# Long convolution by cosine and sine transforms: the transforms folded by parity of time, on one core

## What is computed

```python
h = (sin(...) @ w3 + b3).reshape(L, HY_ORDER, 2, HY_WIDTH) * window   # filters, forward and backward
f = concatenate([fwd, zeros, bwd[1:][::-1]]); f = f / (sum(abs(f)) + EPS)
spec = jnp.fft.rfft(f, axis=0)                                        # length 2 L
y = jnp.fft.irfft(jnp.fft.rfft(u, n=2 * L) * spec, n=2 * L)[:, :L]    # long_conv(u, spec, skip)
return y + u * skip
v, x1, x2 = split(short_conv(u, conv_w), 3)                           # hyena_mixer
z = x1 * long_conv(v, spec[:, 0], skip[0]);  return x2 * long_conv(z, spec[:, 1], skip[1])
```

## Time and profile before

| | us |
|---|---|
| median of three runs | 3444.6 |
| lowest, highest | 3440.48, 3444.97 |
| profiled execution | 3438.63 |
| its span | 3436.7 |
| TensorE busy | 3308.8 (96%) |
| VectorE busy | 2126.0 (62%) |
| ScalarE busy | 1777.6 (52%) |
| GpSimd busy | 636.9 (19%) |
| mean granted TensorE clock | 0.983 |

### The profile page before, as it was taken

The page is one execution under the profiler, slowest core; times in us unless marked ns, Lnnn a source line. Parts: engine busy times, 40 slices in busy tenths (PEclk is TensorE's granted clock), DMA queues, the critical chain, the costliest instruction groups (busy, mean ns, idle before and its releaser), DMA issues.

```text
span 3436.7 us, 55376 instructions
## 1 busy us (share of the span) xinstructions
PE 3308.8 (96%) x22902; PEld 3047.7 (89%) x22902; DVE 2126.0 (62%) x3208; ACT 1777.6 (52%) x2712; POOL 636.9 (19%) x260
## 2 busy tenths in 40 slices
PE   6889999999999889999999999999999999999999
PEld 6879999998888779999998887888999979899998
DVE  7754956657777556946655555575655456755544
ACT  4434556664444545556654554455455445555562
POOL 0000886660000003976640000000000000000000
PEclk8979999999999999999999999999999999999999
DMA  7343554448887333554456655332534634244355
GB/s 254 129 141 117 160 181 143 139 148 274 278 276 261 129 125 127 180 166 140 142 178 194 197 191 184 129 127 97 186 136 158 186 107 143 86 172 168 120 178 135
DMA packets 263693, 565.53 MB, mean 165 GB/s; under 512 B 15438, under 2 KB 93714, under 8 KB 262674
## 3 DMA queue, kind: packets, MB, share of 16 engines
q1 hardware_dynamic: 263444, 561.99, 50.0%
HBM read 560.89 MB, written 1.05 MB: 164 GB/s over the span
## 4 chain that ended last, share of the span: by engine, by line
PE 84%; DVE 7%; ACT 3%; DMA 3%; POOL 2%; issue 1%; SPq 0%; DVEq 0%; ACTq 0%
PE ps L372 8%; PE ps L1888 8%; PE ps L374 7%; PE ps L1889 7%; PE ps L373 7%; PE ps L1890 7%; PE ps L1970 6%; PE ps L1972 6%; PE ps L1971 6%; PE ps L1936 3%; PE ps L402 3%; POOL uvr_split L2288 2%; PE ps L404 2%; DVE ring_split L471 1%; PE ps L528 1%
## 5 line engine op out<-in xcount | busy, mean ns | idle before, releaser
L2288 POOL TENSOR_TENSOR uvr_split<-uvr,high_split 128x1024 fp32r<-128x1024 f32 x172 | 432.4, 2517 | 1057.8 <-ACT high_split L2017 1057.8
L1890 PE MATMUL ps<-consts_sb_split,uvr_split 128*128 128x256 f32 x2048 | 579.1, 283 | 0.0
L2017 ACT ACTIVATE high_split<-uvr 128x1024 fp32r<-128x1024 f32 x342 | 360.8, 1056 | 235.8 <-PE ps L1972 182.0
L374 PE MATMUL ps<-uvr_split,ring_split 128*128 128x256 f32 x1680 | 476.9, 284 | 0.0
L1889 PE MATMUL ps<-ht_split,high_split 128*128 128x256 f32 x1488 | 423.8, 285 | 0.0
L1888 PE MATMUL ps<-consts_sb_split,high_split 128*128 128x256 f32 x1392 | 403.4, 290 | 6.7 <-DVE ht_split L603 3.8
L471 DVE TENSOR_TENSOR ring_split<-big,high_split 128x2048 fp32r<-128x2048 f32 x111 | 251.8, 2268 | 250.2 <-ACT high_split L463 249.5
L471 DVE TENSOR_TENSOR ring_split<-big,hot_split 128x2048 fp32r<-128x2048 f32 (+2 forms) x111 | 248.6, 2240 | 253.0 <-ACT hot_split L463 252.3
L1971 PE MATMUL ps<-uvr_split,hot_split 128*128 128x512 f32 x1024 | 398.5, 389 | 0.0
L1890 PEld LDWEIGHTS ps<-consts_sb_split,uvr_split 128*128 128x128 f32 x2048 | 392.0, 191 | 0.0
L374 PEld LDWEIGHTS ps<-uvr_split,ring_split 128*128 128x128 f32 x1680 | 323.1, 192 | 0.0
(11 more groups left out here) (462 smaller groups left out, 8433.6 us busy)
## 6 DMA issues: line engine op xcount, KB each, us to landing
uvr<-peer_uv SPq DMA_DIRECT2D x512, 512.0 KB, 4.2
big<-mlp_w SPq DMA_DIRECT2D x32, 2048.0 KB
big<-w_in SPq DMA_DIRECT2D x26, 2048.0 KB
uvr<-mod_w SPq DMA_DIRECT2D x56, 512.0 KB, 6.6
big<-peer_w_q SPq DMA_DIRECT2D x8, 2048.0 KB
big<-hy_w_in SPq DMA_DIRECT2D x6, 2048.0 KB
big<-mod_w SPq DMA_DIRECT2D x24, 512.0 KB, 4.1
big<-mod_w SPq DMA_DIRECT2D x8, 1024.0 KB
```

The source lines that it names most:

```text
L374: m = mm(out, wl, x_high[:, k, :], start=False, stop=en)
L1890: return mm(out, w_low, x_high, start=False, stop=stop, **kw)
L2288: GE.tensor_tensor(expert_low(j), expert(j), expert_high(j).bitcast(F32), ALU.subtract)\
```

## The change

Time steps are taken by parity: "half" `t` of a tile no longer means steps 128 t to 128 t + 127, but even (0) or odd (1) steps. For frequency k and its mirror 255 - k, the sum over even steps is equal and the sum over odd steps changes its sign (cosine; for the sine the even sum changes its sign, and the inverse undoes it). So one product with half of the table is made for each parity, and the sum and the difference of the two results give both halves of the frequencies. The inverse makes sums and differences first, and then one product for each parity of time. Tables shrink to half and are padded to the same size; nothing in the DMA list changes.

What it adds and removes: L2509 and L2684 go from two accumulated products for each (part, k) to one for each (part, parity); the odd one goes to a bank of the pool "act", which ScalarE empties, the even one to a bank of the pool "dve", which VectorE reads directly. L2695 keeps its number of products, each of 128 columns instead of 256. ScalarE empties two banks where it emptied four. VectorE gets `folded_dve` (two instructions on 128x512) for each part, and `sums_by_parity` (two more) for each part of a convolution. The filter functions, transposes and last additions read or write `h2` and `u0` with a step of two elements.

```diff
+        def by_parity_pe(part, src, name):
+            for t, pool in ((1, "act"), (0, "dve")):
+                b = acquire(pool)
+                mm(ps[:, b, :], h_fwd[:, t, part, :], src[t], start=True, stop=True).then_inc(S[filled[pool]], 1)
+                frees(b, "odd_times" if t else name)
+
+        def folded_dve(out, name):
+            even, odd = take("dve"), out[:, 1, :]
+            VE.wait_ge(S["odd_times"], S.nth(VE, "odd_times"))
+            VE.tensor_tensor(out[:, 0, :], even, odd, ALU.add).then_inc(S["dve_step"], 1)
+            VE.tensor_tensor(odd, even, odd, ALU.subtract).then_inc(S[name], 1)
+            VE.wait_ge(S["dve_step"], S.nth(VE, "dve_step"))
+            VE.wait_ge(S[name], S.nth(VE, name))
...
 def filter_pe:
-                    mm(ps[:, b, :], z.h2[0:65, t * P:(t + 1) * P], w[0:65, n * 512:(n + 1) * 512], start=True,
+                    mm(ps[:, b, :], by_parity(z.h2[0:65, :])[:, t, :], w[0:65, n * 512:(n + 1) * 512], start=True,
...
-                    for k in range(2):
-                        b = acquire("act")
-                        for t in range(TM):
-                            m = mm(ps[:, b, :], h_fwd[:, t, part * T + k * P:part * T + (k + 1) * P], src[:, t, o, :],
...
+                    by_parity_pe(part, [src[:, t, o, :] for t in range(TM)], "spectra")
...
 def filter_act:
             magnitudes(2)
-            evict_act(spectra[:2], frees="spectra", n=2)
+            evict_act([z.F[:, 0, w, 1, :] for w in range(2)], frees="odd_times", n=2)
             magnitudes(3)
-            evict_act(spectra[2:4], frees="spectra", n=2)
             split_x_act(h, z.h_high, "h_part")
-            evict_act(spectra[4:], frees="spectra", n=4)
+            evict_act([z.F[:, 1, w, 1, :] for w in range(2)], frees="odd_times", n=2)
...
 def filter_dve:
             block_norm_dve(z.rs, V["ln_mix"][:, 8 * L:8 * L + 8], name="h_part")
+            for w in range(2):
+                folded_dve(z.F[:, 0, w], "spectra")
             magnitudes(2)
             magnitudes(3)
+            folded_dve(z.F[:, 1, 0], "spectra")
             split_x_dve(h, h_low, z.h_high)
+            folded_dve(z.F[:, 1, 1], "spectra")
             split_low()
...
-            VE.wait_ge(S["spectra"], S.nth(VE, "spectra", 8))
...
 def mixers_pe:
-                            for k in range(2):
-                                m = mm(ps[:, b, (c - c0) * T:(c - c0 + 1) * T], z.Y[:, part, k, c * P:(c + 1) * P],
-                                       h_inv[:, 2 * part + k, :], start=(part == 0 and c == c0 and k == 0),
...
+                            for t in range(TM):
+                                at_ = (c - c0) * T + t * P
+                                m = mm(ps[:, b, at_:at_ + P], z.U[:, part, t, c * P:(c + 1) * P],
+                                       h_inv[:, part, t, :], start=(part == 0 and c == c0 and t == 0),
...
 def mixers_act:
-                evict_act([z.U[:, w, k, :] for w in range(2) for k in range(2)], frees="u_spectrum", n=4)
+                evict_act([z.U[:, w, 1, :] for w in range(2)], frees="odd_times", n=2)
...
 def mixers_dve:
-                VE.wait_ge(S["u_spectrum"], S.nth(VE, "u_spectrum", 2))
+                folded_dve(Ur, "u_spectrum")
                 VE.tensor_tensor(z.Y[:, 0], Ur, Fr, ALU.mult).then_inc(S["dve_step"], 1)
                 VE.tensor_tensor(z.Y[:, 1], Ur, Fi, ALU.mult).then_inc(S["dve_step"], 1)
-                VE.wait_ge(S["u_spectrum"], S.nth(VE, "u_spectrum", 2))
+                folded_dve(Us, "u_spectrum")
                 VE.tensor_tensor(z.t1, Us, Fi, ALU.mult).then_inc(S["dve_step"], 1)
                 VE.wait_ge(S["dve_step"], S.nth(VE, "dve_step", 3))
-                VE.tensor_tensor(z.Y[:, 0], z.Y[:, 0], z.t1, ALU.add).then_inc(S["y_spectrum"], 1)
...
+                VE.tensor_tensor(z.Y[:, 0], z.Y[:, 0], z.t1, ALU.add).then_inc(S["dve_step"], 1)
...
+                def sums_by_parity(part):
+                    VE.tensor_tensor(z.U[:, part, 0], z.Y[:, part, 0], z.Y[:, part, 1],
+                        ALU.add).then_inc(S["dve_step"], 1)
+                    VE.tensor_tensor(z.U[:, part, 1], z.Y[:, part, 0], z.Y[:, part, 1],
+                        ALU.subtract).then_inc(S["y_spectrum"], 1)
...
+                sums_by_parity(0)
                 VE.tensor_tensor(z.t1, Us, Fr, ALU.mult).then_inc(S["dve_step"], 1)
                 VE.wait_ge(S["dve_step"], S.nth(VE, "dve_step"))
-                VE.tensor_tensor(z.Y[:, 1], z.t1, z.Y[:, 1], ALU.subtract).then_inc(S["y_spectrum"], 1)
...
+                VE.tensor_tensor(z.Y[:, 1], z.t1, z.Y[:, 1], ALU.subtract).then_inc(S["dve_step"], 1)
...
+                sums_by_parity(1)
```

More of the change, by code:

```diff
@@ L89, in constant_tables @@
     th = 2 * np.pi * (np.arange(T)[None, :] + 0.5) * np.arange(T)[:, None] / (2 * T)
-    fwd = np.concatenate([np.cos(th), np.sin(th)], 1).reshape(TM, P, 2 * T)
-    inv_ = (np.concatenate([np.cos(th), np.sin(th)], 1).T / T).reshape(4, P, T)
+    waves = np.stack([np.cos(th), np.sin(th)], 0)[:, :, 0:P].reshape(2, P, TM, P)
+    fwd = waves.transpose(1, 2, 0, 3)
+    inv_ = waves.transpose(3, 0, 2, 1) / T
+    pad = np.zeros((P, 512))
     tn = np.arange(T, dtype=np.float32) / (T - 1)
@@ L97, in constant_tables @@
     winb[0] = 0.0
[L98 to L100 removed]
+    hy = [fwd.reshape(P, -1), pad, inv_.reshape(P, -1), pad, win.reshape(P, -1), winb.reshape(P, -1)]
     w = (2.0 * math.pi * np.arange(T, dtype=np.float32) / T).astype(np.float32)
@@ L2347, in two_blocks @@
         hyc = uvr[:, 0:4096]
-        h_fwd = hyc[:, 0:1024].rearrange("p (m n) -> p m n", m=TM)
-        h_inv = hyc[:, 1024:2048].rearrange("p (k t) -> p k t", k=4)
+        h_fwd = hyc[:, 0:512].rearrange("p (m w k) -> p m w k", m=TM, w=2)
+        h_inv = hyc[:, 1024:1536].rearrange("p (w m t) -> p w m t", w=2, m=TM)
+        by_parity = lambda v: v.rearrange("p (t m) -> p m t", m=TM)
         h_win = hyc[:, 2048:3072].rearrange("p (m n) -> p m n", m=TM)
@@ L2534, in magnitudes @@
                     SE.activation(z.mags[j % 2][k], z.fb[j % 2][k], ACT.Abs).then_inc(S["magnitudes"], 1)
-            spectra = [z.F[:, o, w, k, :] for o in range(2) for w in range(2) for k in range(2)]
             magnitudes(0)
@@ L2671, in mixers_pe @@
                     for c in range(4):
-                        m = TE.transpose(ps[:, b, c * P:(c + 1) * P], z.u0[:, c, t * P:(t + 1) * P], C["ident"])
+                        m = TE.transpose(ps[:, b, c * P:(c + 1) * P], by_parity(z.u0[:, c, :])[:, t, :], C["ident"])
                     m.then_inc(S["tile_for_act"], 1)
@@ L2680, in mixers_pe @@
                 for part in range(2):
-                    for k in range(2):
[L2682 to L2687, removed]
+                    by_parity_pe(part, [z.ut[:, t, :] for t in range(TM)], "u_spectrum")
                 linear()
@@ L2693, in mixers_pe @@
                         for c in (c0, c0 + 1):
-                            for k in range(2):
-                                m = mm(ps[:, b, (c - c0) * T:(c - c0 + 1) * T], z.Y[:, part, k, c * P:(c + 1) * P],
-                                       h_inv[:, 2 * part + k, :], start=(part == 0 and c == c0 and k == 0),
-                                       stop=(part == 1 and k == 1), skip_group_check=True)
+                            for t in range(TM):
+                                at_ = (c - c0) * T + t * P
+                                m = mm(ps[:, b, at_:at_ + P], z.U[:, part, t, c * P:(c + 1) * P],
+                                       h_inv[:, part, t, :], start=(part == 0 and c == c0 and t == 0),
+                                       stop=(part == 1), skip_group_check=True)
                         if part == 1:
@@ L2971, in mixers_dve @@
                         signal = "convolved" if c > c0 else "dve_step"
-                        VE.scalar_tensor_tensor(out=v, in0=t[:, (c - c0) * T:(c - c0 + 1) * T],
-                            scalar=z.sinv[:,
-                            4 * o + c:4 * o + c + 1], in1=v, op0=ALU.mult, op1=ALU.add).then_inc(S[signal], 1)
+                        v = by_parity(v)
+                        VE.scalar_tensor_tensor(out=v, scalar=z.sinv[:, 4 * o + c:4 * o + c + 1],
+                            in0=t[:, (c - c0) * T:(c - c0 + 1) * T].rearrange("p (m t) -> p m t", m=TM), in1=v,
+                            op0=ALU.mult, op1=ALU.add).then_inc(S[signal], 1)
                         VE.wait_ge(S[signal], S.nth(VE, signal))
```

9 lines of the change are left out of this document (4 added, 5 removed).

## The result

The changed kernel takes 3458.68 us (median of six, 3453.04 to 3461.11), the kernel before in the same comparison 3441.99. The ratio is 1.0046 with an interval of 1.0035 to 1.0058: **slower by 0.46%**, 16.7 us. The predicted 3456 was reckoned as 11.5 us over a median of 3444.6, which lies 2.6 us above the median of this larger comparison. The profiled execution took 3457.91 us, its span 3456.1.

What follows compares the result with a forecast made beforehand. VectorE, level with TensorE or ahead as the bound, was taken to set the stages, with waits lowering TensorE's clock. Terms +2.3, +5.65 and 2 x 1.8 made +11.5 us on the 3444.6 median, forecast 3456, range 3438 to 3467.

Steps and rivals of the forecast that it cites:

- What bounds the stages: Filter stages and convolutions: VectorE is level with TensorE or already the bound, so TensorE's saved 40.7 us turn into waits.
- VectorE's price: Each added pair of VectorE instructions costs 1.34 us; 12 pairs a layer, 32.2 us in all.
- The clock: After some 6 us idle, TensorE's sums of magnitudes run wholly at the lower clock, 7.0 us, bounds 3.5 and 7.0.
- The loss behind it: The linear layer after the filter stage starts at the lower clock, losing 2.45 us; new only in layer 1.
- the +1.35 for o = 0: First inverse of each convolution layer ends 1.35 us later; both inverses together +1.8 a layer, bounds +0.5 and +3.4.
- Filter stage: VectorE's pairs delay the magnitudes, TensorE idles, then runs slowly: +2.3 us in layer 0, +5.65 in layer 1.
- The sum: Filter stages +2.3 and +5.65, convolutions 2 x 1.8: +11.5 us in all, added to the median of 3444.6.
- the term of zero: Behind the stages, later waits and delayed weight-piece splits cost nothing; the added time simply carries over.
- The prediction's own range for this case: 3451 with +0.5 a convolution layer and 5 at the filters; 3462 with 3.4 and 1 us more behind each magnitude sum.
- That the clock holds: Rival: waits open in filter stages and convolutions but the clock holds or falls only partly; -3.0 us, 3442, chance 0.20.
- That TensorE's work counts and the kernel gets faster: Rival: saved TensorE work shortens the kernel; all 40.7 us give 3404, the filter stages alone 3431; chance 0.08.
- The step of two: Rival: transposes' and additions' reads with a step of two cost double, at most 12 us more, 3466; chance 0.10.

Runs made afterwards that it cites:

- sums_only: Changed kernel without the second instruction of each VectorE pair, in filter stages and convolutions, output wrong: 3445.63 us against 3439.07 for the kernel before, ratio 1.0014.
- filter_only: Changed kernel folded in the filter stages only, convolutions unfolded with the full inverse of 256 columns: 3452.16 us against 3439.30 for the kernel before, ratio 1.0038.
- conv_only: Changed kernel folded in the convolutions only, filter stages unfolded: 3446.99 us against 3439.30 for the kernel before, ratio 1.0019.
- filled: Changed kernel plus unread products on TensorE during its waits before the sums of magnitudes and the inverses: 3449.98 us against 3439.83 for the kernel before, ratio 1.0037.
- parity_only: Changed kernel with times taken by parity but nothing folded, products as before, steps of two kept: 3439.24 us against 3439.30 for the kernel before, ratio 1.0004.
- before_again: The kernel before, run once more without any edit for a second trace: 3440.73 us against 3439.83, ratio 1.0009.
- late: Changed kernel with ScalarE emptying all filter banks and VectorE's filter sums and differences made after the stage: 3447.73 us against 3439.83 for the kernel before, ratio 1.0022.
- mended: Changed kernel, filter sums made after the stage plus 13 unread products, convolutions unfolded, short convolution's last four channels moved later: 3428.72 us against 3443.55 before, ratio 0.9965.

## Why the prediction was right

**What bounds the stages.** Right. The waits that were to open did, at their places: 5.88 us before the sums of magnitudes (6 predicted), 10.2 and 4.57 at the inverses in both layers (10 and 4.4 predicted). The second wait in each inverse, predicted at about 2 us, was 0.4 or less, since the first part ran at the lower clock. sums_only shows that VectorE's list is the bound, and filter_only and conv_only that the product work saved pays in neither stage.

**VectorE's price.** 1.34 us a pair, 1.38 in the trace.

**The clock.** 7.0 us for L2529 were taken between the bounds of 3.5 and 7.0; it took 6.85. The loss behind it, 2.45 us in layer 1, shows as 2.2 (the shift grows from 12.8 at the piece's start to 15.0 at its end). filled shows that the clock is a cause in the filter stages. Right for those, and wrong for the convolutions: the +1.35 for o = 0 had a share for a slower second part of the inverse, and +0.45 came for o = 1. The second part ran at the upper clock again (2.05 us for o = 1), the stages cost 1.2 and 1.4 us, not 1.8, and with the clock held the cost stayed. That term was over-sized, by 1 us in all.

**Filter stage.** Layer 1: +5.65 predicted, +5.4 in both traces. Layer 0: +2.3 predicted, +2.5 and +1.0 measured against the first trace of before, 5.7 and 4.3 against the second. The prediction took the clock of one execution as the kernel's, and a second execution has another.

**The sum.** 11.5 predicted, 16.7 measured. The four stages add up to 10.5 and 9.0 in the two traces. The rest is what the prediction took as nothing: that behind the stages a shift carries over. From 2347 to 2500 and from 2820 to 2846 another 5.7 and 5.3 us came in, each time as a wait for a weight piece with a stretch at the lower clock behind it. The first of the two also comes without any folding (parity_only); the second comes only in folded versions, though not in all. The longer wait goes with an instruction transfer inside the weight transfer (see before_again); whether that transfer causes it stays open, since it was not tried alone. Part of the 5 us may also be the ruler: between two executions of the kernel before, the filter stages alone differ by -3.3 and +1.5 us. The sum of the terms was right for the stages, the term of zero for what lies behind them was not; the forecast of 3456 came near 3458.68 in part by luck: the difference was 5.2 us too small, and the median that it was added to was 2.6 us too high. The prediction's own range for this case, 3451 to 3462, has 3458.68 in it (its upper end adds up to 3461), but for another reason than the one it gave: the 3.4 us for a convolution layer, which it allowed for, did not come, and the 5 us behind the stages did.

**The rivals.** That the clock holds: no, 71.6 and 68.2 us at the lower clock against 23.8. That TensorE's work counts and the kernel gets faster: no. The step of two: no, within 0.13%.

## What to carry to other kernels

Before halving an engine's work in a stage, read when the other engines' signals to it come: here TensorE, 96% busy, stood level with VectorE in two stages, and the saved products turned into waits of 6 and 10 us while the new additions stood ahead of the signals. If such a trade is wanted, put the new work behind the last signal of the stage (late: 8 us), and look at what TensorE does in the gap, since a wait of 3.12 us was followed by 32 records at half the pace in one layer and at two thirds of it in the other. Check the filler's own waits as one would any step's.

## What was not expected of the hardware

- Thirty-two fp32 records of one column each take 3.49 us at clock 1.00 and 6.85 at 0.50; these short products follow TensorE's clock fully. TensorE counts as busy while they run, and yet the clock fell in the midst of them in filled (0.68), after products at clock 1.00, and in layer 0 of the kernel before. It held through them in mended and in layer 1 of filled.
- A weight load that reads with a step of two elements took 209 ns instead of 140, and eight transposes 0.10 to 0.14 us longer; VectorE's additions with that step took the same time.
- Two executions of the same kernel differed by 3.3 us in one stage of 47 us, by where the lower clock fell; 1.3 us of it came back 20 us later.
- A transfer of 16 KB of instructions, 1 us long, went with a weight transfer that took 8.9 to 9.3 us instead of 7.8 to 8.0 whenever it started in the middle of it.
